# Second block's projections as three single-pass products of high and low parts

## The reference

```python
def second_block(x, c, ctx, c_ctx, ada_w, ...):
    for l in range(L):
        sh1, sc1, g1, sh2, sc2, g2 = ada_params(c, ada_w[l], ada_b[l])        # and the same for c_ctx
        h = modulate(rms_norm_2(x, norm1_g[l]), sh1, sc1)
        hc = modulate(rms_norm_2(cx, norm1_g[l]), csh1, csc1)
        p, pc = h @ w_in[l], hc @ w_in[l]             # 1024 x 2304; the last layer needs only keys and values of pc
        y_a = fourier_mix(p[..., 0:256])
        y_b = neighbourhood_attention(p[..., 256:1024], context keys and values, rpb[l])
        y_c = spatial_gating(p[..., 1024:1536], ...)  # u * (w_s @ layer_norm(v)), u and v through gelu
        y_d = diff_post(diff_latent(p[..., 1536:2304], ...))
        x = x + g1 * (concatenate([y_a, y_b, y_c, y_d]) @ w_out[l])           # and cx in the first layer
        x = x + g2 * sq_relu_mlp(modulate(rms_norm_2(x, norm2_g[l]), sh2, sc2), w_ff1[l], w_ff2[l])
    return rms_norm_2(x, final_g)
```

## Time and profile before

| what | value |
| --- | --- |
| median of 3 runs | 3247.66 us (3245.68 to 3249.27) |
| profiled execution | 3246.96 us |
| its span, first to last instruction | 3245.3 us |
| TensorE busy | 3011.3 us, 93% |
| VectorE, ScalarE, GpSimd busy | 1348.9, 1088.3, 248.5 us |
| mean granted TensorE clock | 0.970 of full speed |
| second block, first layer | about 1392 to 2482 us |
| second block, second layer | about 2482 to 3245 us |

### The profile page before, as it was taken

The page is one execution under the profiler, slowest core; times in us unless marked ns, Lnnn a source line. Parts: engine busy times, 40 slices in busy tenths (PEclk is TensorE's granted clock), DMA queues, the critical chain, the costliest instruction groups (busy, mean ns, idle before and its releaser), DMA issues.

```text
span 3245.3 us, 39893 instructions
## 1 busy us (share of the span) xinstructions
PE 3011.3 (93%) x16068; PEld 2129.5 (66%) x16068; DVE 1348.9 (42%) x2127; ACT 1088.3 (34%) x1869; POOL 248.5 (8%) x334
## 2 busy tenths in 40 slices
PE   7999979979999799989999789999999999879998
PEld 5657855446568754446676558887886576658886
DVE  5665432246655422334234653232333341644434
ACT  4555321134654311142122542222222131543332
POOL 0011010000100200010002210000001001200000
PEclk9999989999999899999999989999999999989999
DMA  3011259951013299953211002322321221012221
GB/s 145 27 40 69 89 204 415 417 228 52 14 47 111 91 400 418 415 226 142 79 53 39 1 34 110 125 109 104 130 80 58 105 78 46 14 52 91 104 91 52
DMA packets 61492, 414.20 MB, mean 128 GB/s; under 512 B 6992, under 2 KB 7504, under 8 KB 13696
## 3 DMA queue, kind: packets, MB, share of 16 engines
q1 hardware_dynamic: 55664, 392.59, 30.8%
q0 software_dynamic: 4496, 16.98, 1.6%
q10 hardware_dynamic: 1152, 2.10, 0.2%
HBM read 409.53 MB, written 2.10 MB: 127 GB/s over the span
## 4 chain that ended last, share of the span: by engine, by line
PE 85%; DVE 7%; DMA 3%; ACT 3%; issue 2%; POOL 1%; DVEq 0%; SPq 0%; ACTq 0%; POOLq 0%
PE banks L726 82%; PE banks L727 3%; DVE arena L2068 3%; DMA weight<-in_w_up 3%; ACT arena L1464 2%; DVE arena L2655 1%; DVE weight_part L2172 0%; DVE arena L2347 0%; DVE tokens_low L2068 0%; DVE x L2068 0%; DVE arena L2345 0%; POOL arena L2761 0%; ACT weight_part L1464 0%; DMA mats<-in_k_mats 0%; DVE arena L2119 0%
## 5 line engine op out<-in xcount | busy, mean ns | idle before, releaser
L1464 ACT ACTIVATE arena<-banks 128x512 f32<-128x512 f32 (+4 forms) x528 | 293.5, 560 | 1188.6 <-PE banks L726 1036.8
L726 PE MATMUL banks<-weight,arena 128*64 128x512 f32 (+5 forms) x2808 | 574.4, 527 | 27.1 <-ACT arena L1464 13.0
L726 PEld LDWEIGHTS banks<-weight,arena 128*64 128x64 f32 (+2 forms) x2808 | 268.6, 145 | 296.6 <-issue 262.0
L726 PE MATMUL banks<-hidden,weight_part 128*128 128x512 f32 (+1 forms) x2304 | 446.4, 355 | 0.0
L726 PE MATMUL banks<-arena,weight 128*128 128x512 f32 (+1 forms) x1120 | 422.7, 533 | 20.9 <-DVE arena L2068 10.7
L726 PE MATMUL banks<-tokens_high,weight_part 128*128 128x512 f32 (+1 forms) x1536 | 419.8, 359 | 22.9 <-DVE tokens_low L2068 22.8
L726 PEld LDWEIGHTS banks<-hidden,weight_part 128*128 128x128 f32 x2304 | 381.0, 189 | 70.3 <-issue 3.5
L726 PEld LDWEIGHTS banks<-arena,weight 128*128 128x128 f32 x1120 | 211.3, 193 | 212.5 <-issue 186.0
L726 PEld LDWEIGHTS banks<-tokens_high,weight_part 128*128 128x128 f32 x1536 | 275.7, 191 | 82.1 <-DVE tokens_low L2068 29.5
L726 PE MATMUL banks<-tokens_low,weight_part 128*128 128x512 f32 (+1 forms) x768 | 274.1, 357 | 0.0
L2172 DVE TENSOR_TENSOR weight_part<-weight,weight_part 128x2048 fp32r<-128x2048 f32 x98 | 225.1, 2300 | 86.7 <-ACT weight_part L1464 86.5
(11 more groups left out here) (198 smaller groups left out, 3208.1 us busy)
## 6 DMA issues: line engine op xcount, KB each, us to landing
weight<-in_w_gate SPq DMA_DIRECT2D x64, 1024.0 KB, 13.6
weight<-in_w_up SPq DMA_DIRECT2D x64, 1024.0 KB, 8.2
weight<-in_w_down SPq DMA_DIRECT2D x64, 1024.0 KB, 10.8
weight<-in_w_ff SPq DMA_DIRECT2D x64, 1024.0 KB, 4.8
weight<-in_ada_w SPq DMA_DIRECT2D x48, 1024.0 KB, 5.1
weight<-in_w_in SPq DMA_DIRECT2D x28, 1024.0 KB, 7.6
weight<-in_w_o SPq DMA_DIRECT2D x8, 1024.0 KB, 4.8
weight<-in_w_mem_kv SPq DMA_DIRECT2D x8, 1024.0 KB, 4.8
```

The lines of the kernel that those rows point to most:

```text
L726: mm = lambda o, a, b, first=True, last=True: eng.matmul(o, a, b, start=first, stop=last, skip_group_check=True)
L1464: act = lambda o, i, f=ACT.Copy, **k: eng.activation(o, i, f, **k)
```

## The change

1. All nine projections and four output projections of each layer use `tile3` or `joint3` on high and low parts. Their weights are split as the others are (`IN_BLOCK`), ACT first, DVE behind. `split_high` and `split_low` calls are written into the two queues by hand.
2. The tokens' high part (`HI`) lies in the weight slots 5 to 7 for as long as the projections need it; the low part (`HT`) lies in the arena. ACT writes the high part (`block_high`), DVE the low part of x (`block_low`), POOL that of the context (`context_low`), for which ACT writes the shifted context tokens a second time.
3. So in the second block raw projection weights use slots 0 to 2, high parts of weights 3 and 4; feat, cos_n, sin_n, w_s and the ada chunks of q = 1, 2 may use 0 to 4. In the feed-forward stage raw weights use 0, 1, 2, 5, 6, 7 and high parts 3 and 4. dft_c is loaded with feat in the first layer.
4. The branch outputs get a high part (`YH`, ACT) and a low part (`YL`, DVE).
5. The ada chunks of q = 1 stand three ahead of fa (`AHEAD`) and one behind each tile of su and sv; those of q = 2 one behind each tile of nq and nk.
6. nq moves ahead of sg, nk and `out_proj(2)` ahead of na, which has no filler any more; `out_proj(1)` stands beside df's units 4 to 7 (`BESIDE`).
7. The squares of "fin1" stand on ACT between `block_high` and the copies of fa. In the last expert pairs of the first block's second layer loads may use all eight slots.

The diff, cut to its core:

```diff
+            def conditioned(q, a, b):
                 if l == 0:
-                    for k in range(KD):
+                    for k in range(a, b):
                         ada_chunk(l, q, k)
-
-            conditioned(0)
 
             def cols(name, c):
                 packed((name, l), "w_in_2", (l,), c // 256, KD, 256)
@@ -430,24 +433,31 @@
             def outs(g):
                 packed(("w_out", l, g), "w_out_2", (l,), g, 2, 1024)
 
+            if l == 0:
+                for k in range(KD):
+                    ada_chunk(0, 0, k)
             cols("w_four", 0)
-            conditioned(1)
             fo = A["k_fourier"]
-            o = 2 * TB * T + 4 * CT
-            chunk(("feat", l), fo[:, o:o + 256], 256)
+            o = 2 * TB * T
+            conditioned(1, 0, AHEAD)
+            if l == 0:
+                chunk(("feat", l), fo[:, o:o + 4 * CT + 256], 4 * CT + 256)
+            else:
+                chunk(("feat", l), fo[:, o + 4 * CT:o + 4 * CT + 256], 256)
             chunk(("cos_n", l), fo[:, 0:TB * T], TB, T)
             chunk(("sin_n", l), fo[:, TB * T:2 * TB * T], TB, T)
-            if l == 0:
-                chunk(("dft_c", l), fo[:, 2 * TB * T:o], 4, CT)
             cols("w_u", 1024)
+            conditioned(1, AHEAD, AHEAD + 4)
             cols("w_sv", 1280)
+            conditioned(1, AHEAD + 4, KD)
             outs(0)
-            conditioned(2)
+            cols("w_nq", 256)
+            conditioned(2, 0, 4)
             chunk(("w_s", l), A["sgu_wT"][l], 4, P)
-            cols("w_nq", 256)
             cols("w_nk", 512)
+            conditioned(2, 4, KD)
+            outs(2)
             cols("w_nv", 768)
-            outs(2)
...
+        BLOCK_LOADED, BLOCK_HIGH = (0, 1, 2), (3, 4)
+        is_split = lambda key: key[0] in ("w_in", "w_o", "w_mkv", "w_mq", "w_mo", "ff1", "ff2") + IN_BLOCK
+        IN_BLOCK = ("w_four", "w_u", "w_sv", "w_nq", "w_nk", "w_nv", "w_dv", "w_dq", "w_dk", "w_out")
+
+        def fills(key):
+
+            if key[0] in ("w_gate", "w_up", "w_down") and not (key[2] == PAIRS - 1 and key[0] != "w_gate" and key[1] == 0) or key[:3] == ("ada", 0, 0):
+                return range(NW)
+            if key[0] in ("ff1", "ff2") or key in [("w_out", l, g) for l in range(L) for g in (1, 3)]:
+                return BLOCK_LOADED + HI_SLOTS
+            if key[0] in IN_BLOCK:
+                return BLOCK_LOADED
+            if key[:2] == ("ada", 1):
+                return BLOCK_LOADED + HI_SLOTS
+            if key[0] in ("feat", "cos_n", "sin_n", "w_s", "ada"):
+                return BLOCK_LOADED + BLOCK_HIGH
+            return LOADED
+
+        def fills_high(key):
+            return BLOCK_HIGH if key[0] in ("ff1", "ff2") + IN_BLOCK else HIGH_SLOTS
+
+        hi_former = {}
         slot_of, former_of, high_of, high_former, loads, holder = {}, {}, {}, {}, [0] * NW, [(-1, None)] * NW
         for n, key in enumerate(load_order):
-            i = min(range(NW) if may_fill_all(key) else LOADED, key=lambda z: holder[z][0])
+            if key[0] == "w_four":
+                hi_former[key[1]] = [holder[z][1] for z in HI_SLOTS]
+            if key[0] == "w_out" and key[2] == 1:
+                for z in HI_SLOTS:
+                    holder[z] = (n - 1, ("hi_dead", key[1]))
+            i = min(fills(key), key=lambda z: holder[z][0])
             slot_of[key], former_of[key] = i, holder[i][1]
             holder[i] = (n, WF(key))
             loads[i] += 1
             st.put(("w", key), (f"w{i}", 16 * loads[i]))
             if is_split(key):
-                i = min(HIGH_SLOTS, key=lambda z: holder[z][0])
+                i = min(fills_high(key), key=lambda z: holder[z][0])
                 high_of[key], high_former[key] = i, holder[i][1]
                 holder[i] = (n, WF(key))
...
+                HX, HC = [[(S["HI"][:, k, cols], S["HT"][:, k, cols]) for k in range(KD)] for cols in (slice(0, T), slice(T, T + CT))]
+
+                def project(key, name, js=range(2), ctx_too=True, w=None, then=None, free=None):
+
+                    w = weight_parts((name, l)) if w is None else w
                     for j in js:
+                        end = (WF((name, l)),) + ((free,) if free else ()) if j == 1 else ()
+                        tile3((key, l, j), halves(w, j), HX, free=() if ctx_too else end)
+                        if then:
+                            then()
                         if ctx_too:
+                            tile3((key, l, j, "c"), halves(w, j), HC, CT, free=end)
+                            if then:
+                                then()
                     return w
 
+                def project_rows(key, name, nb, then=None):
+                    w = weight_parts((name, l))
                     for c in range(nb):
+                        tile3((key, l, c), [(S["HI"][:, k, c * P:c * P + P], S["HT"][:, k, c * P:c * P + P]) for k in range(KD)],
+                              [(w[0][:, k, :], w[1][:, k, :]) for k in range(KD)], 256, free=(WF((name, l)),) if c == nb - 1 else ())
+                        if then:
+                            then()
 
...
+                rest = {1: list(range(AHEAD, KD)), 2: list(range(KD))}
+
+                def some(q):
+
+                    return (lambda: rest[q] and ada(0, q, rest[q].pop(0), PO)) if both else None
+
+                project("su", "w_u", ctx_too=both, then=some(1))
+                project_rows("sv", "w_sv", nb, some(1))
+                if both:
+                    ada_turn(0, 1, PB)
                 out_proj(0)
-                if both:
-                    for k in range(KD):
-                        ada(0, 2, k, PO)
+                project("nq", "w_nq", ctx_too=both, then=some(2))
...
+                project("nk", "w_nk", then=some(2))
+                out_proj(2)
...
+            def block_high(l, S):
+
+                H, HI = S["H"], S["HI"]
+                for r, tag in enumerate((("n1x", l), ("n1c", l))):
+                    cols = slice(0, T) if r == 0 else slice(T, T + CT)
+                    for k in range(KD):
+                        eng.wait_ge(*after(("h", tag, k)))
+                        act(HI[:, k, cols], H[:, k, cols], ACT.Identity, bias=ADA[l][:, k, r:r + 1]).then_inc(*done(("hh", tag, k)))
+                eng.wait_ge(scalar_step, done.count)
+                for k in range(KD):
+                    act(H[:, k, cols], H[:, k, cols], ACT.Identity, bias=ADA[l][:, k, 1:2]).then_inc(*done(("hs", tag, k)))
...
                         gelu_in(*keys[i])
                     if i:
                         gelu_mid(*keys[i - 1])
+                    if i == first_sv:
+                        split_high(("w_out", l, 0))
+                    if both and i == first_sv + 2:
+                        ada_rows(0, 1, PO)
+                split_high(("w_nq", l))
                 exp_set()
...
+                split_high(("w_nk", l))
                 for j in range(2):
                     high("QH", ("nq", l, j), 64 ** -0.5, j, 0)
                     if both:
                         high("QH", ("nq", l, j, "c"), 64 ** -0.5, j, 1)
+                split_high(("w_out", l, 2))
+                branch_high(2)
                 for j in range(2):
                     high("KH", ("nk", l, j), 1.0, j, 0)
                     high("KH", ("nk", l, j, "c"), 1.0, j, 1)
+                split_high(("w_nv", l))
+                if both:
+                    ada_rows(0, 2, PO)
+                split_high(("w_dv", l))
...
+                    if i == 1:
+                        eng.wait_ge(*after(("hi_dead", l)))
+                        branch_high(1)
+                    if i == 2:
+                        split_high(("w_out", l, 1))
+                    if i == len(us) // 2:
+                        split_high(("w_out", l, 3))
+                    if i == len(us) // 2 + DF_POST + 2:
+                        branch_high(3, [0])
...
+            def block_low(l, S):
+
+                for k in range(KD):
+                    eng.wait_ge(*after(("hh", ("n1x", l), k)))
+                    stt(S["HT"][:, k, 0:T], S["H"][:, k, 0:T], ADA[l][:, k, 0:1], S["HI"][:, k, 0:T], ADD, SUB).then_inc(*done(("h2", ("n1x", l), k)))
...
+                def branch_low(g, js=range(2)):
+
+                    for j in js:
+                        for i in range(1 + both):
+                            cols = (slice(0, T), slice(T, T + CT))[i]
+                            eng.wait_ge(*after(("yh", l, g, j, i)))
+                            tt(S["YL"][:, j, cols], S["YG"][:, j, cols], S["YH"][g][:, j, cols], SUB).then_inc(*done(("y2", l, g, j, i)))
...
+                split_low(("w_out", l, 2))
+                branch_low(2)
+                begun = meet(("na", l))
+                for j in range(2):
+                    low("KL", "KH", ("nk", l, j), 1.0, j, 0)
+                    low("KL", "KH", ("nk", l, j, "c"), 1.0, j, 1)
+                split_low(("w_nv", l))
...
+            def context_low(l):
+
```

(4 more changed lines are left out.)

253 lines of the change are left out of this document (138 added, 115 removed).

## The result

The changed kernel takes 3268.91 us (median of 4 runs, 3266.41 to 3270.21) where the kernel before took 3248.47 in the runs beside it: a ratio of 1.0059 (95% interval 1.0048 to 1.0071). It is slower by 0.59%, 20 us. That lies inside the forecast range of 3220 to 3279 and beyond the 6.5 us that a measurement can tell, on the side that had the largest single chance; the likeliest case's own figure of 3249 with 3237 to 3260 was missed by 9 us at its upper end.

The account below looks back on a forecast made before the run. Full-precision products on TensorE in the projections were taken as the bound. Layer changes of +23.7 and -22.8 us sum to +1: 3248 on the profiled execution, 3249 as the runs' median; range 3220 to 3279.

Parts of the forecast that it names:

- Rates of the products: Projections: three single-pass products at feed-forward rates, 0.683 us per 512 columns and 0.36 per 256; a pair 1.043 against 1.30.
- The four waits of the first layer: Before sv, in sv and out0, before nk, before out2: waits for slots or banks of 10.9, 6.4, 10.9, 13.2 us; sum 41.4.
- Rival (a): First-layer loads wait as said, but other work keeps TensorE busy: whole 3201, chance 0.08; half 3225, chance 0.14.
- The clock behind the idle times: First layer, su to na: work behind each of four stalls runs slower, 2 us each time, 6.5 us in all.
- Head of the first layer: Up to su's end: uv at 1440, su at 1463.6, su ending at 1482.9 in place of 1483.57.
- na: Neighbourhood attention: start waits 0.9 us without fillers, w_dq's split adds 3.6; +4.5 us in each layer.
- dv, dq, dk: Projections between na and df: dv saves 3.6 us per layer, dq and dk 8.3 in the first, 7.1 in the second.
- df to the feed-forward stage: Differential attention through out3: added splits and branch parts cost +4.5 and +4.6 us, plus clock +1.5 per layer.
- rival (b): In na and df, splits and branch parts lie wholly on the path: +16 to +22 us, 3269; chance 0.28.
- Second layer before na: su to nv save 22.2 us and idle time of 2.72 goes: -22.7 us net.
- two sums: Whole kernel: two sums of opposite sign, each ten times the difference; a fifth's error in either leaves "same".
- Rival (c): GpSimd's eight context low parts wait for VectorE's 2.30 us split instructions at w_u: +3 us a layer, 3255; chance 0.03.

## Why the prediction was right in its causes and 20 us off in its size

*Rates of the products.* Right. Two lines of su after, seven steps apart:

```profile
1469.00 0.39 PE L764 MATMUL banks<-block_tokens_low,weight_part 128*128 128x512 f32 x1
...
1473.78 0.39 PE L764 MATMUL banks<-block_tokens_low,weight_part 128*128 128x512 f32 x1
```

(1473.78 - 1469.00) / 7 = 0.683 us, the feed-forward rate of the earlier trace rows. By the rule of the Trainium skill, "FP8 and Floating Point Precision", section "TensorE Precision Notes", three of four passes of the measured 0.869 would have been 0.65, an estimate; the trace does not agree.

*The four waits of the first layer.* Right in all four places and in the releasers: three behind a slot, one for banks. 36.6 us of idle time against 41.4 forecast (9.6, 5.8, 9.3 and 11.9 against 10.9, 6.4, 10.9 and 13.2; the terms written for the first of them give 10.6, not 10.9). Putting the loads in another order gave 35 back. Rival (a), that other work covers the stalls, is excluded by the 11.54 us with 1.92 of work in them.

*The clock behind the idle times* is the term that was mis-sized. From su's end to na's start the forecast has 1644 - 1482.9 = 161.1 us: 41.4 of stalls, 6.5 for half clock and so 113.2 of work; TensorE is busy 130.47 us, 10.8 more than the last two. Of the 130.47, 26.5 us ran at 1.2 GHz. At full clock they would be up to 13 us shorter, twice the 6.5. I had priced each stall at 2 us, which the filled stalls confirm (1.8 and 2.2), but counted four, where seven idle times of 3.75 to 7.15 us cost clock. The other 4 us are work at full clock: an ada chunk among tiles takes 1.04 us in place of the 0.88 of the earlier trace rows, 1.6 us for ten of them, and the rest is not explained. In the order without these stalls TensorE is busy 122.62 us at 0.96.

The same term is short in the whole second block: 122.0 us of TensorE's work ran at 1.2 GHz there, 56.5 in the kernel before. Half of the difference, 33 us, is the most that this can cost; where stalls were filled, 4.1 and 4.9 us of such work gave 1.8 and 2.2 back, which makes it some 29. The forecast had 6.5 + 1.5 + 1.5 = 9.5. So this one term is some 20 us short, as much as the forecast's total is; all the others together, idle time and work at full clock, come within 3 us of it.

*Head of the first layer.* uv started at 1440.73, 1439.3 on the clock of before (the whole block began 1.45 us later): forecast 1440. Its idle time of 8.61 us was not priced, and uv ran at half clock for most of its 8.35 us; so su started 3.5 us later than forecast, and its three ada chunks made it 1.3 us longer, some 5 us in all. Taken together na's start came at 1656.16 - 1.45 = 1654.7 in place of 1644.

*na.* First layer +5.1 against 4.5 (54.55 in place of 70.91 less four fillers, 49.5; +5.4 with dv's first product as the border); second +8.2 against 4.5 (48.38 in place of 54.64 less four fillers of 3.6). Moving the one split gave back 6.7 there. The step had the split's own 3.6 us, and not the clock behind it.

*dv, dq, dk.* -11.0 (-11.4 from dv's first product) against -11.9 (59.79 for 70.79) and -10.2 against -10.7. Right.

*df to the feed-forward stage.* +7.9 and +7.8 against +6.0 and +6.1: the mechanism of rival (b), in small. Its price of 16 to 22 us beyond the forecast did not come (3.6 did, with 4.3 in na); that the total landed on its 3269 is the sum of other terms, and luck. Its sign of being wrong, df and na longer by over 5 us each, is met in all four stretches if it is counted from the kernel before (5.1, 7.9, 8.2 and 7.8); but the forecast itself has 4.5 and 6.0 there, so the sign as it was written could hardly tell the two apart.

*Second layer before na.* -21.8 against -22.7. Right; the feed-forward stages moved by under 0.2 us each, right too.

Sum by the traces: 1.45 ahead of the block (not explained, and within what two executions differ by), +37.9 and -16.0 for the layers against +23.7 and -22.8. Of the 21.0 us that this is above the forecast for the layers, 10.7 lie ahead of na in the first layer. The forecast calls its two sums ten times their difference. They are larger than that, 94 us saved and some 95 paid for a difference of 1, and 21 us is a fifth of either: what decided the sign was an error of the size that it had warned of.

*Rival (c).* GpSimd took 5.59 us for eight parts, 0.70 each, while VectorE had nothing to do: the split of w_u came only at 1465.80, since its high part waits for cos_n's slot. In the second layer VectorE was idle beside the eight parts too (5.50 us). So these runs do not test the port; the rival's price did not come because the two never met.

## What to carry to other kernels

Before a change that takes buffer slots away, write down for each load whose release it waits for, and what is queued behind it: here loads that waited for the projection now running cost load, split and half clock in full, and another order of the same loads took 35 us of it away. A piece of work that passes through two engines belongs in two different steps, or beside a stretch in which both are idle. Add about 2 us of half clock to each of the longer idle times of TensorE (here those of 3.7 to 8.6 us) when a sum is made.
